# Attention in groups of two head pairs, with turns and values one group behind the scores

## What is computed

```python
# first block, each of 2 layers: 8 heads of 64, three branches per head
ss = q @ k * 64**-0.5; ps = softmax(where(mask, ss, NEG)); o_s = ps @ v
out = g[..., 0] * o_c + g[..., 1] * o_s + g[..., 2] * o_w
# second block, layer 0: dense attention (8 heads) and a window with a sink (8 heads)
# second block, layer 1: neighbourhood attention with a bias (8 heads),
#                        latent attention (8 heads, scores from 64 + 32 rows)
# second block, both layers: cross attention to a memory of 256 tokens (4 heads of 128)
x = x + mixed @ w_out
```

## Time and profile before

| what | value |
|---|---|
| median of three runs | 2277.22 us (2274.36 to 2278.72) |
| span of the profiled execution | 2275.0 us |
| its own time beside the span | not given; the span is 2.2 us under the median |
| PE busy | 2199.9 us (97%) |
| DVE, ACT, POOL busy | 1246.9, 1078.0, 853.7 us |
| mean granted TensorE clock | 0.989 |

### The profile page before, as it was taken

How to read it: one execution, slowest core, us unless ns; L and a number is a source line. 1 busy time by engine, 2 the same in 40 slices (tenths; PEclk the granted TensorE clock), 3 DMA queues, 4 the chain that set the end, 5 groups by cost and what they waited for, 6 DMA issues and landing times.

```text
span 2275.0 us, 33281 instructions
## 1 busy us (share of the span) xinstructions
PE 2199.9 (97%) x12130; PEld 1763.7 (78%) x12130; DVE 1246.9 (55%) x2614; ACT 1078.0 (47%) x2160; POOL 853.7 (38%) x665
## 2 busy tenths in 40 slices
PE   8999899999999999989999999999999999999997
PEld 6778667888866788668888888888767888888886
DVE  6997782499778446885552112234666655211222
ACT  6542484465247652685453223343566545322332
POOL 4333304443330343104255545554110425554553
PEclk9999899999999999999999999999999999999998
DMA  5334002332410233203233333343110323333331
GB/s 171 85 91 141 25 2 79 104 91 79 144 38 11 75 89 109 68 2 110 67 94 96 95 109 98 92 124 95 48 60 20 111 66 97 94 95 100 98 96 66
DMA packets 107186, 189.74 MB, mean 83 GB/s; under 512 B 12049, under 2 KB 22801, under 8 KB 106897
## 3 DMA queue, kind: packets, MB, share of 16 engines
q1 hardware_dynamic: 101136, 178.67, 27.3%
q10 hardware_dynamic: 5888, 8.95, 1.2%
HBM read 182.85 MB, written 2.10 MB: 81 GB/s over the span
## 4 chain that ended last, share of the span: by engine, by line
PE 85%; DVE 10%; issue 3%; ACT 2%; POOL 1%; DMA 0%; SPq 0%; DVEq 0%; ACTq 0%
PE bank L861 23%; PE bank L863 23%; PE bank L862 23%; PE bank L1090 3%; PE bank L1103 3%; PE bank L1076 2%; DVE temp L1933 1%; DVE bank L2053 1%; PE bank L868 1%; DVE temp L1965 1%; PE bank L1067 1%; PE bank L1070 1%; PE bank L931 1%; DVE temp L1967 1%; POOL w_lo L2212 1%
## 5 line engine op out<-in xcount | busy, mean ns | idle before, releaser
L2212 POOL TENSOR_TENSOR w_lo<-w_raw,w_hi 128x512 fp32r<-128x512 f32 (+3 forms) x618 | 824.7, 1341 | 1337.1 <-ACT w_hi L1226 1336.7
L861 PE MATMUL bank<-op_hi,w_hi 128*128 128x512 f32 x1840 | 734.4, 399 | 9.1 <-POOL w_lo L2212 4.4
L863 PE MATMUL bank<-op_hi,w_lo 128*128 128x512 f32 x1840 | 719.4, 391 | 0.0
L862 PE MATMUL bank<-op_lo,w_hi 128*128 128x512 f32 x1840 | 719.4, 391 | 0.0
L1226 ACT ACTIVATE w_hi<-w_raw 128x512 fp32r<-128x512 f32 (+2 forms) x634 | 385.4, 617 | 682.5 <-PE bank L863 678.8
L861 PEld LDWEIGHTS bank<-op_hi,w_hi 128*128 128x128 f32 x1840 | 347.1, 189 | 95.7 <-issue 15.3
L862 PEld LDWEIGHTS bank<-op_lo,w_hi 128*128 128x128 f32 x1840 | 347.6, 189 | 73.4 <-issue 4.1
L863 PEld LDWEIGHTS bank<-op_hi,w_lo 128*128 128x128 f32 x1840 | 347.1, 189 | 73.7
L1648 DVE TENSOR_TENSOR temp<-bank,rstd 128x512 f32<-128x512 f32 x151 | 104.4, 691 | 396.0 <-PE bank L863 378.2
L861 PE MATMUL bank<-side_hi,w_hi 128*128 128x512 f32 (+1 forms) x628 | 233.2, 371 | 2.5 <-DVE side_lo L1730 1.4
L863 PE MATMUL bank<-side_hi,w_lo 128*128 128x512 f32 (+1 forms) x628 | 230.9, 368 | 0.0
(11 more groups left out here) (269 smaller groups left out, 2256.3 us busy)
## 6 DMA issues: line engine op xcount, KB each, us to landing
w_raw<-in_weights SPq DMA_DIRECT2D x620, 256.0 KB, 2.7
w_raw<-in_weights SPq DMA_DIRECT2D x32, 192.0 KB, 2.3
temp<-temp SPq DMA_DIRECT2D x40, 64.0 KB, 2.0
x_t<-in_x SPq DMA_DIRECT2D x8, 256.0 KB, 5.4
conv_area<-in_mem ACTq DMA_DIRECT2D x2, 1024.0 KB, 5.5
out_y<-ybuf SPq DMA_DIRECT2D x8, 256.0 KB, 2.1
conv_area<-in_bias ACTq DMA_DIRECT2D x1, 1920.0 KB, 8.0
conv_area<-in_bias ACTq DMA_DIRECT2D x2, 960.0 KB, 4.9
```

The source lines that it names most:

```text
L861: pe.matmul(dst, w[0], m[0], start=start, stop=False)
L862: pe.matmul(dst, w[0], m[1], start=False, stop=False)
L863: return pe.matmul(dst, w[1], m[0], start=False, stop=stop)
L2212: pool.tensor_tensor(w_lo[:, j, 0:n], w_raw[:, p % RAW_RING, 0:n], w_hi[:, j, 0:n].bitcast(F32), ALU.subtract).then_inc(*mark("weights_spl ...
```

## The change

For all stages but X2, two pairs form a *group* of four tiles. PE has at step `s` the scores of group `s`, then the four turns and the two pairs of values of group `s-1`. ACT has the exponents of three tiles of group `s`, the copy of the first tile of group `s-1`, the exponent of the fourth tile, and the three other copies. DVE has the scaling of the first pair of group `s-1`, the maxima of the first pair of group `s`, the same for the second pairs, and the output of group `s-1`.

The score banks are always 1, 2, 3, 0. The turns of a group go to banks 4, 5, a third one, and 4: outside NSA the third is the bank that the group's values will be written to, in NSA bank 4 and later 7 (the order is then 4, 5, 4, 5, or 4, 5, 7, 4). `E` has eight buffers instead of six; the fourth `PT` buffer is `rstd`. An output is taken for two query blocks at once (128x256). The layer norm and the last gate strip move from bank 0 to bank 7. X2 keeps its lags of 2 and 3 pairs.

```diff
-TURN_LAG = 2
-VALUE_LAG = 3
-OUT_LAG = 7
+PAIRS = {"NSA": 2, "AB2": 2, "D2": 2, "C2": 2, "X2": 1}
+TURN_LAG = {1: 2, 2: 1}
+VALUE_LAG = {1: 3, 2: 1}
...
-E_RING = 6
+E_RING = 8
...
-GATE_CHUNKS = (2, 1, 1, 4)
+GATE_CHUNKS = (2, 2, 4)
...
+                        third = t["out"] if step[1][0] != "NSA" else 7 if n >= LN_TILES else 4
+                        t["turn"] = (4, 5, third, 4 if third != 4 else 5)[n % 4]
...
 # PE, values(pair)
                         pe.wait_ge(*after("probs_copied", t["a"]))
+                        if t["first"] and t["size"] == 4:
+
+                            pe.wait_ge(*after("probs_copied", t["a"] + 2))
...
 # PE
+                for s in range(steps_of(part)):
+                    for pair in in_group(groups, s):
+                        scores(pair)
...
+                    for pair in in_group(groups, s - turn_lag):
+                        for t in pair:
+                            turn(t)
+                    for pair in in_group(groups, s - value_lag):
+                        values(pair)
...
 # ACT
+                        for t in to_exp[:3]:
+                            exps(t)
+                        for t in to_copy[:1]:
+                            copy(t)
+                        for t in to_exp[3:]:
+                            exps(t)
+                        for t in to_copy[1:]:
+                            copy(t)
...
 # DVE
+                        for p in range(2):
+                            for pair in before[p:p + 1]:
+                                normed(pair)
+                            for pair in now[p:p + 1]:
+                                for t in pair:
+                                    maxed(t)
+                        for t in [pair[1] for pair in in_group(groups, s - value_lag)]:
+                            if t["last"]:
+                                output(t)
```

More of the change, by code:

```diff
@@ L461, in build @@
         hs, hm, vcb = [tmp(6), tmp(7)], tmp(5), tmp(9)
[L462 removed]
+        krb = ybuf[:, 10, :]
         E = [tmp(i) for i in range(E_RING)]
[L464 removed]
+        PT = [tmp(E_RING), tmp(E_RING + 1), tmp(E_RING + 2), rstd[:, :]]
         gbuf = [tmp(0), tmp(1)]
@@ L593, in build @@
         ATT, Y_GROUP, at_tile, at_group = {}, {}, 0, 0
-        held = {}
+        held, turned = {}, {}
         for step in PROGRAM:
@@ L600, in build @@
                     t["a"], t["g"] = at_tile, at_group
-                    banks = SCORES if step[1][0] == "NSA" and at_tile - ts[0]["a"] < LN_TILES else SCORES + (0,)
-                    t["bank"] = banks[(at_tile - ts[0]["a"]) % len(banks)]
+                    n = at_tile - ts[0]["a"]
+                    t["bank"] = SCORES[n % len(SCORES)]
                     t["held"] = held.get(t["bank"])
@@ L606, in build @@
                     t["first"], t["last"] = t["pos"] == 0, t["pos"] == t["size"] - 1
+                    t["out"], t["out_held"] = (6, at_group - 1) if step[1][0] == "NSA" else (6 + at_group % 2, at_group - 2)
+                    t["turn"] = 4 + n % 2
+                    if PAIRS[step[1][0]] == 2:
+                        third = t["out"] if step[1][0] != "NSA" else 7 if n >= LN_TILES else 4
+                        t["turn"] = (4, 5, third, 4 if third != 4 else 5)[n % 4]
+                    t["turn_held"] = turned.get(t["turn"])
+                    turned[t["turn"]] = at_tile
                     at_tile += 1
@@ L1046, in scores @@
                             pe.wait_ge(*after("maxed", t["held"]))
-                        if part[0] == "NSA" and t["a"] == ts[LN_TILES]["a"]:
-                            pe.wait_ge(*after("ln_scaled", (part[1], 3)))
-                    if part[0] == "C2" and pair is pairs[0]:
+                    if part[0] == "C2" and pair is first:
                         pe.wait_ge(*after("rope_keys", 0))
@@ L1094, in value @@
                     a, r = t["a"], t["r"]
-                    out = bank[6 + t["g"] % 2]
+                    out = bank[t["out"]]
                     last = b == len(t["pv"]) - 1
@@ L1123, in values @@
                                 value(t, b)
-                pairs = [ts[i:i + 2] for i in range(0, len(ts), 2)]
-                for i in range(len(ts) + OUT_LAG + 1):
-                    if i % 2 == 0:
-                        s = i // 2
-                        if s < len(pairs):
-                            scores(pairs[s])
-                        if part[0] == "NSA" and s < 3:
-                            for _ in range(GATE_CHUNKS[s + 1]):
-                                next(begun[LAST_GATE[part[1]]])
-                        if len(pairs) <= s < len(pairs) + 3:
-                            drain(part, steps[s - len(pairs)])
-                        if TURN_LAG <= s < len(pairs) + TURN_LAG:
-                            for t in pairs[s - TURN_LAG]:
-                                turn(t)
-                        if VALUE_LAG <= s < len(pairs) + VALUE_LAG:
-                            values(pairs[s - VALUE_LAG])
-                    for stage in between.get(i, ()):
-                        extra_stage(*stage)
+                groups = groups_of(part)
+                first = groups[0][0]
+                turn_lag, value_lag = lags_of(part)
+                for s in range(steps_of(part)):
+                    for pair in in_group(groups, s):
+                        scores(pair)
+                    if part[0] == "NSA" and s + 1 < len(GATE_CHUNKS):
+                        for _ in range(GATE_CHUNKS[s + 1]):
+                            next(begun[LAST_GATE[part[1]]])
+                    if 0 <= s - len(groups) < 3:
+                        drain(part, steps[s - len(groups)])
+                    for pair in in_group(groups, s - turn_lag):
[3 more added lines that the diff above has]
+                        values(pair)
+                    for i in moments_of(part, s):
+                        for stage in between.get(i, ()):
+                            extra_stage(*stage)
                 drain(part, steps[3])
@@ L1427, in copy @@
                     act.wait_ge(*after("probs_turned", a))
+                    if part[0] == "NSA" and a == ts[PT_RING - 1]["a"]:
+                        act.wait_ge(*taken(LAST_GATE[part[1]]))
                     if a >= PT_RING:
@@ L1972, in output @@
                     dve.wait_ge(*after("values", t["a"]))
-                    o = bank[6 + g % 2][:, 0:T if t["gate"] is not None else P if w == HD else 2 * P]
+                    o = bank[t["out"]][:, 0:T if t["gate"] is not None else 2 * P]
                     if t["gate"] is not None:
```

137 lines of the change are left out of this document (86 added, 51 removed).

## The result

The changed kernel takes 2536.73 us (median; 2535.76 to 2539.64) against 2277.19 for the kernel before: ratio 1.114, 95% interval 1.1125 to 1.1156. It is slower, as forecast, but by 260 us and not by 152: the time lies 37 us above the upper end of my range, and close to the 2527 of the third rival, the clock that stays low. The profiled span is 2537.8 us, the mean granted clock 0.927 instead of 0.989.

What follows compares the result with a forecast made beforehand. PE was taken as the bound by throughput, with grouping adding a serial loop; AB2 53, D2 25, C2 11, NSA 48 and clock 15 us sum to 152 on a span of 2275.0, giving 2429 us; range 2335 to 2500.

Steps and rivals of the forecast that it cites:

- the third rival: Clock stays low in the grouped stages: 113 us instead of 15, 2527 us; half of the time 2471; chance 0.15.
- What bounds the kernel, and the saving on PE: PE bounds by throughput; fewer switches between scores, turns and values save 0.37 us a group, 25 us over 68 groups.
- The loop: Values of one group precede the next scores on PE, making each step a serial chain: 9.4 us per group, not 5.9.
- rival 2: The loop binds but DVE is not on it: dense groups 7.4 us instead of 9.4; 2347 us; chance 0.12.
- Rivals 1, 2 and 4: Loop does not bind, 2252 us, chance 0.07; DVE not on the loop, 2347, 0.12; gain and loop cancel, 0.03.
- NSA's own term: Groups in the two NSA stages take 6.5 us; 24 us added per stage, 48 for both.
- The clock: PE's waiting lowers the clock: seven more of 68 groups at the low level, about 2.1 us each, 15 us.
- the judged 6 and 3 us: NSA's first two head pairs: gate strip and layer norm waits hide part of 9.6 us, leaving 6 and 3 added.
- D2 and C2: The loop lengthens D2 to 80 us, 25 more than 55.3, and C2 to 80, 11 more than 69.1.
- X2, weights, GpSimd and SP: X2 keeps its lags, weight copies fall into ACT's waits, GpSimd and SP only move weights: nothing added.
- DVE's split: In AB2 seven splits of outputs stand on the chain, about 0.60 us each before DVE is free: 4.2 us.
- The test I set: The forecast is wrong if, among other signs, the added time lies outside the five stages.

Runs made afterwards that it cites:

- the orders mended: Changed kernel with ACT's copies first, PE's turns before next scores, DVE's first maxima before scalings, DVE's operand split a group later: 2323.65 us; NSA also as before: 2276.63 us.
- light fill: Changed kernel plus single unused matmuls in PE's waits: at up to four places with an added wait, 2496.07 us; at two places outside NSA without it, 2519.05 us.
- ACT's order: Changed kernel with all four copies of the older group ahead of the newer group's exponents on ACT, nothing else moved: 2388.55 us, ratio 1.049.
- the later split: DVE's low part of each operand split put one group later: 2323.65 us with ACT, PE and DVE reordered, 2362.99 us with only ACT reordered.
- heavy fill: Changed kernel plus unused matmuls in PE's waits, nine per group in AB2, D2 and C2, fewer in NSA, with an added output-bank wait: 2614.5 us, ratio 1.1479.

## Why the prediction was wrong, point by point

- **What bounds the kernel, and the saving on PE**: right. 0.37 us a group were forecast, 0.4 came where PE was left without waits. That it shortens the kernel by as much was wrong. For the 32 groups of AB2, D2 and C2 it makes 12 us; with the orders mended the three stages came out 11 us shorter, but the strips behind them start only 1.4 us earlier, since strips used to run in the drain of the last pairs.
- **The loop**: right in mechanism, place and, for AB2, size. Its chain of 9.4 us shows as 9.5 at the full clock (light fills), and ACT's order in it as 148 us with what the clock gives back. DVE's part shows in its waits for the values and as 9.5 us where rival 2 had 7.4; the price of the output alone is not shown. Rivals 1, 2 and 4 fall with that.
- **What is missing, by terms.** The strips show 262 us where the sum had 152. Of the 110 us between them NSA's own term has about 53, the clock about 37, and the loop in AB2, D2 and C2 about 20 (6, 5 and 9). With the first put right the time would lie in my range, with the second at its edge.
- **The clock: the step that failed.** "Of the 68 groups I count seven more than now at that level: 15 us." The count was a guess from one stretch: half of the stages' time fell to the lower level, and every group of AB2 after the first two has 3.8 us or more of it. The price of a group was about right: such a group costs 1.5 us more in AB2 if dense (11.0 instead of 9.5), where 2.1 were forecast, and 1.1 if of the window (9.7 instead of 8.6), where 1.3 were. Taken at half, rival 3's own working gives 56 us. Measured: AB2 171 against at most 152 at the full clock, D2 92 against at most 84, C2 90 against 85: 32 us, and 10 us for each NSA in the light fill. So 52 us or more, since the fills' own cost is inside, instead of 15. I had reasoned that PE's busy share would stay near what it was before the fall, and then counted as if it had not fallen; the same row should have made rival 3 the forecast, or at least half of it. That the time came out near rival 3's 2527 is in part luck: its 113 us for the clock are twice what the fills gave back, and its other terms hold NSA at 24.
- **NSA: the term that was mis-sized most.** 24 us a stage forecast, 60 to 62 measured, of which the clock explains 10 or more. The groups after the norm (312.8 to 393.9) lasted 9.0 us with two thirds of them at the lower level; 7.0 were forecast (31.5 for a head pair's 4.5 groups), and in the light fill, with little of the lower level, they took 8.1. The judged 6 and 3 us for gate strip and layer norm were too small as well: the ninth group started 22 us late. With all orders mended, it still starts 59.5 us after the first instead of 47.0, and the later groups lose 6 us in place of 34. The end was to be 4 shorter; instead the strips wait there 4.9 us for the last split (L891 on L1635). By the starts of the strips behind it, what NSA adds (61.0 and 60.0 us) falls to 31 and 30 with ACT's order alone, clock included, to 24 and 23 with the later split, to 22 and 23 with PE's and DVE's orders, to 4 and 9 in steps of one pair, and to 2 and less than nothing with the banks and the fill at tile 30 as before. So half of NSA's loss went with ACT's order, which my sum of 6.5 us had in it; which of its terms was too short stays open.
- **D2 and C2**: 38.3 and 24.7 us instead of 25 and 11, of which the clock has about 8 and 5. Steps with bias scalings took 13.6 us, half of it at the lower clock, and 11.9 in the light fill, where 9.4 and 2.3 had been summed. C2's middle groups took 10.0 at the full clock (9.64 forecast); the two ahead of them, partly at the lower clock, 12.9 and 12.7.
- **X2, weights, GpSimd and SP**: nothing, as forecast. DVE's split was priced at its length, and in AB2 of the changed kernel it has no wait ahead of it; the wait for ACT behind the exponents came with the mended orders.
- The test I set, added time outside the five stages, finds 1.6 us, in the first 30 us of the run, which the change does not touch.

## What to carry over

When steps are merged on in-order engines, what decides is which instruction of the older group stands behind which of the newer one on each engine. What worked here was: on ACT the older group's copies ahead of the new exponents, on PE its turns ahead of the new scores and its values behind them, on DVE a pair of maxima ahead of the scalings and the output last, with the lags counted again in the new step. One engine's order changed alone can be worth nothing or less, as PE's was (0 as the sum of 37 us gained in NSA and 33 lost in D2 and C2, then +60 us on top of ACT's); so look at each stage and not at the total alone. And once a loop leaves TensorE waiting, price its low clock for the whole stretch and not for a few groups, since the loop makes the condition last.

## What was not expected of the hardware

- An unused fp32 matmul of 512 columns appears as two passes 0.43 us apart at the full clock, 0.86 us in all (heavy fill).
- Time at the lower clock is not time lost at a fixed rate: 90 us less of it brought 17.7 us in one run (0.20 us each, with the fill's own cost inside) and 291 us less 41 in another (0.14). The rows fit the reading that PE waits for part of that time at either level. The Trainium skill ("TensorE: Matmul & The Clock Gate", Terms) counts the extra time as half of the throttled time. By that rule the 319 us added would cost 160, an estimate, and the 88.7 us in AB2 44; AB2 is 19 us longer than in the light fill at the full clock.
- In NSA an unused matmul raised the stage's clock from 0.86 to 0.94 and made it 13 us longer.
